# A two-layer attention, WKV and mixture-of-experts block and a diffusion block: semaphores of a stage cleared during the next stage

## The reference

```python
def first_block(x, ...):                       # 528 tokens: 16 meta tokens and x
    h = _layer_norm(concatenate([meta, x]), emb_ln_g, emb_ln_b)
    for li in range(2):
        proj = h @ w_in[li]
        c_q, c_kv, k_pe, rw = _split(proj, ...)
        y_att = _mla(c_q, c_kv, k_pe, ...)
        u = _centred_shift(rw, ...)
        y_rwkv, v_first = _rwkv_bidir(u, v_first, ...)
        mixed = concatenate([y_att, y_rwkv]) @ w_out[li]
        h = _layer_norm(DN_ALPHA * h + mixed, ...)
        ff = _hier_moe(h, ...)                 # 32 experts, two per token
        h = _layer_norm(DN_ALPHA * h + ff, ...)
    return h[:, N_META:]

def second_block(x, c, ctx, ...):
    h_lat = rms_norm(x, norm_mix) * (1 + m_lat[1]) + m_lat[0]
    ...
    ya = window_attn(...); yb = global_attn(...); yc = hgrn2_bidir(...)
    x_mix = x + m_lat[2] * merge_branches(ya, yb, yc, gates, w_branch, w_out)
    h = rms_norm(x_mix, norm_ffn) * (1 + m_lat[4]) + m_lat[3]
    return rms_norm(x_mix + m_lat[5] * conv_ffn(h, ...), norm_final)
```

## Time and profile before

| | |
|---|---|
| time, median of 3 runs | 3746.04 us (3744.92 to 3749.94) |
| the profiled execution, first to last instruction | 3735.3 us |
| PE busy | 3204.0 us, 86% |
| DVE busy | 1687.3 us, 45% |
| mean granted clock of TensorE | 0.927 of full speed |
| stages run | 20 |
| `mix_in`, layer 0 and 1 (end of second barrier to end of second barrier) | 277.5 and 282.3 us |
| `rwkv_prep` | 55.3 and 53.8 us |
| `wkv` | 302.5 and 309.1 us |
| `mix_close` | 112.4 and 111.5 us |
| `route` | 29.6 and 29.6 us |
| `experts` | 278.4 and 279.7 us |
| `combine` | 44.9 and 44.0 us |
| `scale_inputs`, `attend`, `branch_attention`, `gated_scan`, `close` | 30.9, 113.0, 301.5, 240.7, 750.9 us |

### The profile page before, as it was taken

One profiled execution on the slowest core, in us unless ns is written; L12 is line 12 of the kernel. 1 busy time (PEld: TensorE's weight loads), 2 busy tenths in 40 slices (PEclk: granted clock), 3 DMA queues, 4 the chain that ended last, 5 costly groups with the idle time before them and its releaser, 6 DMA issues. The chain is left out here.

```text
span 3735.3 us, 75687 instructions
## 1 busy us (share of the span) xinstructions
PE 3204.0 (86%) x32538; PEld 2376.1 (64%) x32538; DVE 1687.3 (45%) x3124; ACT 876.1 (23%) x1808; POOL 373.7 (10%) x530
## 2 busy tenths in 40 slices
PE   4899799986873899799986873989998899999998
PEld 0666599864442666699764442557656688878843
DVE  2344455543113344355542115445457776566611
ACT  3122322212113112323121114133353311022200
POOL 0000121001111000121001112000025400000000
PEclk7999799997996999799998996999999999999999
DMA  8210300209996110300219994110010032222221
GB/s 320 70 46 28 139 5 5 82 15 357 392 404 172 34 34 27 137 5 5 82 59 359 390 395 123 34 47 24 29 52 1 10 115 79 91 68 91 77 70 46
DMA packets 175437, 421.93 MB, mean 113 GB/s; under 512 B 25795, under 2 KB 122435, under 8 KB 146579
## 3 DMA queue, kind: packets, MB, share of 16 engines
q1 hardware_dynamic: 156147, 383.22, 27.8%
q0 software_dynamic: 8736, 17.32, 1.8%
q10 hardware_dynamic: 10240, 16.79, 1.3%
HBM read 400.55 MB, written 50.54 MB: 121 GB/s over the span
## 5 line engine op out<-in xcount | busy, mean ns | idle before, releaser
L2052 PE MATMUL ps<-e_w,e_xt 128*64 128x256 f32 x1792 | 225.7, 408 | 68.6 <-DMA e_w<-in_moe_w 67.1
L2052 PEld LDWEIGHTS ps<-e_w,e_xt 128*64 128x64 f32 x1792 | 148.8, 148 | 166.7 <-issue 78.1
L732 PE MATMUL ps<-h,win 128*128 128x264 f32 x960 | 232.8, 396 | 17.2 <-DVE pad L881 15.6
L732 PEld LDWEIGHTS ps<-h,win 128*128 128x128 f32 x960 | 180.4, 193 | 67.7 <-issue 39.1
L2159 DVE TENSOR_TENSOR e_hid<-ps,e_silu 64x256 f32<-64x256 f32 x64 | 39.4, 616 | 401.8 <-ACT e_silu L2118 401.8
L3548 PE MATMUL ps<-ff_up,wt 128*128 128x512 f32 x352 | 152.2, 592 | 0.0
L3488 PE MATMUL ps<-h_lat,wt 128*128 128x256 f32 x544 | 133.4, 388 | 15.0 <-DMA wt<-in_w_in 8.3
L1440 DVE COPY_PREDICATED inv<-level,ps 112x384 f32<-112x384 int32 x176 | 103.3, 587 | 83.2 <-PE ps L1341 74.4
L1341 PE MATMUL ps<-inv,nt 48*48 48x48 f32 x3520 | 131.4, 207 | 6.8 <-issue 5.7
L3488 PE MATMUL ps<-h_lat,w_sums 128*128 128x256 f32 x544 | 130.1, 382 | 0.0
L2071 PE MATMUL ps<-e_w,e_hid_t 128*64 128x512 f32 x448 | 110.8, 613 | 20.5 <-DMA e_w<-in_moe_w 16.9
(11 more groups left out here) (621 smaller groups left out, 6880.0 us busy)
## 6 DMA issues: line engine op xcount, KB each, us to landing
e_w<-in_moe_w SPq DMA_DIRECT2D x168, 1024.0 KB
wmod<-in_w_mod SPq DMA_DIRECT2D x24, 1024.0 KB, 14.3
early<-in_moe_w SPq DMA_DIRECT2D x24, 1024.0 KB, 13.4
wt<-in_w_up SPq DMA_DIRECT2D x22, 1024.0 KB, 5.1
y_rows<-e_y ACTq DMA_DIRECT2D x128, 128.0 KB
win<-in_w_in SPq DMA_DIRECT2D x10, 1536.0 KB, 6.6
wt<-in_w_in SPq DMA_DIRECT2D x12, 1024.0 KB, 5.1
wt<-in_w_down SPq DMA_DIRECT2D x16, 704.0 KB, 4.6
```

The costliest lines, as they stand in the source:

```text
L732: last = pe.matmul(ps[:, 7, 0:HT], lhsT=ring[(s + 1) % 2][:, i, o:o + P], rhs=k.h[:, i, h * HT:(h + 1) * HT], start=(i == 0), stop=(i == K ...
L2052: last = pe.matmul(ps[half, 2 + z, 0:EH], lhsT=xt[z][:, f, :], rhs=w[:, f, :], start=(f == 0), stop=(f == KD - 1))
```

## The change

A stage no longer has a `clear` block of its own, unless it must. Its semaphores are kept in `k.spent` until the next stage ends. That stage adds, behind SP's own code, a second stretch for SP that clears them one by one, and then closes its block with the one barrier. The next stage's semaphores have other numbers, because the old ones are given back only then. Stages that keep the old form (one barrier, the clears dealt out, a second barrier) are those that use the fixed set or semaphores that outlive them (`experts`, `combine`, `attend`, `gated_scan`) and those marked `settle=True` (`prelude`, ahead of the loop, and `close`, the last). The seven others are `mix_in`, `rwkv_prep`, `wkv`, `mix_close` and `route`, run twice, and `scale_inputs` and `branch_attention`, run once.

```diff
@@ class Stage @@
     def __exit__(self, *exc):
+        k = self.k
+        pool = [s for n, s in zip(self.names, self.sems) if n in k.pool_sems]
+        sems = [s for n, s in zip(self.names, self.sems) if n not in k.pool_sems] + self.also
+        spent, k.spent = k.spent, None
+        if exc[0] is None and spent is not None:
+            @self.b.sync
+            def _(sp):
+                for s in spent[0]:
+                    sp.sem_clear(s)
         self.block.__exit__(*exc)
+        if spent is not None:
+            spent[1].__exit__(None, None, None)
+        if exc[0] is None and not (pool or self.also or self.settle):
+            k.spent = (sems, self.stack)
+            return
         if exc[0] is None:
-            with self.k.nc.Block() as clear:
-                pool = [s for n, s in zip(self.names, self.sems) if n in self.k.pool_sems]
-                sems = [s for n, s in zip(self.names, self.sems) if n not in self.k.pool_sems] + self.also
+            with k.nc.Block() as clear:
```

More of the change, by code:

```diff
@@ L117, in __init__, with stage @@
         self.pool_sems = {}
+        self.spent = None
     def sb(self, name, shape, dt=F32, stack=None, side="left"):
         return (stack or self.top).enter_context(self.nc.sbuf_tensor(name, shape, dt, side=side))
-    def stage(self, *names, also=()):
-        return Stage(self, names, also)
+    def stage(self, *names, also=(), settle=False):
+        return Stage(self, names, also, settle)
     def pool_dma_sems(self, *names):
@@ L131, with __init__ @@
 class Stage:
-    def __init__(self, k, names, also=()):
-        self.k, self.names, self.also = k, names, list(also)
+    def __init__(self, k, names, also=(), settle=False):
+        self.k, self.names, self.also, self.settle = k, names, list(also), settle
     def __enter__(self):
@@ L353, in prelude @@
                      "strip_turned", "modded", "gained", "pre_chain", *[f"x_in{j}_" for j in range(NC1)],
-                     *[f"wmod_in{i}" for i in range(RING)]) as (
+                     *[f"wmod_in{i}" for i in range(RING)], settle=True) as (
                 block, blanked, consts_in, par_in, pos_in, pos_set, grid_in, c_done, ps_clear, centred, emb_squared, emb_root,
@@ L3435, in close @@
                  "x_scaled", "hl_made", "side_made", "silu_done", "gated", "f_squared", "f_summed", "f_root",
-                 "f_scaled", "o_turned", "o_kept", "o_stored", "dve_chain", *[f"w_in{z}" for z in range(RING)]) as (
+                 "f_scaled", "o_turned", "o_kept", "o_stored", "dve_chain", *[f"w_in{z}" for z in range(RING)],
+                 settle=True) as (
             block, p6_made, p7_made, p3_made, made, p1_kept, split, t_made, u2_made, u34_made, assembled, posted,
```

## The result

The changed kernel takes 3727.35 us (median of 4 runs, 3721.26 to 3729.23) against 3745.48 for the kernel before in the same comparison (4 runs, 3741.45 to 3749.94). The ratio is 0.995, with a 95% interval of 0.9938 to 0.9963.

A forecast was written before the change was run, and what follows sets the result against it. It took the seams between stages, where all five engines stand still, as on the path whichever engine bounds a stage. Seams 11.9 less `route` 0.6 gave 11.3 us off 3746.0: 3734.7 us, range 3729.5 to 3740.0.

The forecast's parts named there:

- The seams' sum: At twelve of 20 stage ends, the stretch from first to second barrier release on PE goes: 11.9 us saved.
- The cost in `route`: SP's 21 added clears stand behind its wait for stores, making SP last at the barrier in layer 0: 0.6 us.
- The lower bound: In `route`, added cost 0 if the stores land some 1.2 us ahead of DVE in both layers.
- The covers: In the stages other than `route`, SP reaches the barrier early, so its added clears cost nothing.
- The first rival: Behind `wkv`, shorter PE idle time keeps the clock up in `mix_close`: 4.2 us more saved, 3730.5 us; chance 0.13.
- The second rival: In `wkv`, clock drops shift both layers into the worse pattern: 6.6 us lost, 3741.3 us; chance 0.14.
- The third rival: At the twelve seams, the pause had covered code fetch: 1.2 us each, 14.4 us cost, 3749.1 us; chance 0.03.
- From span to median: For the whole run, the median of runs was taken as 10.7 us above the profiled execution, 3735.3 us.
- What it named as its own test: Over all stages, the prediction is wrong if the sum of lengths falls by under 7.5 us or over 16.

The follow-up runs named there:

- Experiment 2: Kernel before with every seam's clears done twice: 3759.09 us, ratio 1.0034; changed kernel with an empty second barrier kept at twelve seams: 3736.31 us, 0.998; repeated 3740.13, 0.9981.

## Why the prediction was right or wrong, point by point

**The seams' sum, 11.9 us: right.** It measured 12.2, and the 0.3 between is rounding. Experiment 2 shows that such a microsecond counts as one.

**The cost in `route`, 0.6 us: it measured nothing.** SP, with its 21 clears, was at the barrier 0.7 and 1.2 us ahead of DVE in the first trace of the changed kernel and 0.4 to 1.4 us ahead of the release in all eight `route` ends of four traces. The clears did cost SP 1.2 us, as reckoned; but the stores that it waits for landed earlier against DVE than in the two places of the earlier trace rows. Why they did was not tried. The lower bound, 0, was the right end.

**The covers: right.** SP's clears vanish in `rwkv_prep`, `wkv`, `mix_close`, `attend`, `gated_scan` and `experts`: in the first trace of the changed kernel SP is at these barriers 16 us or more ahead of the release. `experts` moved by 0.6 us.

**The first rival, the clock gives more back: right in kind, and the step that failed.** It was priced at 4.2 us in one stage, given a chance of 0.13 and kept out of the forecast. `mix_close` gave back 3.0 of these 4.2. What was missing is the second place: the earlier trace rows looked at the short stretch behind one seam, and I had not looked behind the others. The 2.7 us of `rwkv_prep` had a sign in the kernel before, in whose trace its two runs start at 0.54 and 0.66 with 54.4 and 52.7 us. The argument used against it, that the last matmuls of `wkv` are thin anyway, is no reason: they were as thin after. The mis-sized term is thus the clock's share, taken as 0 in the forecast, where 7.6 ± 1.1 us were measured by the means and 6.5 ± 1.3 by the ratios. Some 0.6 of it is the shorter time outside the span, and 5.7 are found in the two stages; the rest has not been traced.

**The second rival, the clock takes some: refuted for the median.** `wkv` stayed at 300.7 to 302.3 us in layer 0 of all four traces of the changed kernel and took 301.0 to 309.5 in layer 1, so both layers at 309 never came; it is scatter, as the prediction itself argued against it.

**The third rival, code fetch: refuted.** At each of the twelve seams of the changed kernel, in all four traces, some engine is at work within 0.1 us of the release. PE is at eight of them; at the end of `mix_in` it starts after 0.7 us and at that of `route` after some 11, both as in the kernel before.

**From span to median: a step that was wrong and hid itself.** The forecast took the profiled execution's distance from the median, 10.7 us, as a constant. That execution took some 3738 us with the time outside its span, 10 below the mean of 3747.6; the changed kernel's profiled execution is 3721.26 against a mean of 3727.6. Both lie at the low end of the scatter. Since only the difference of 11.3 was laid on the median, the error did no harm here; but stretches read from such a trace are those of a short execution, perhaps with fewer starts at the lower clock than the mean has.

**What it named as its own test**, a sum of the stages' lengths that falls by over 16 us, was just not met by the profiled pair (15.9), and was met by the mean spans of all executions (19.4).

## What to carry to other kernels

A pause in which all engines stand still costs its whole length, which is read from release to release, and it can cost again, by the clock that PE has behind it: look at the granted clock and the length of the first 10 to 15 us behind every such pause, in all instances of the stage, and where the same stage starts at different clocks, price each seam with that difference before giving it a small chance. Clear semaphores with one instruction over a range of numbers, or where the engine has time; dealing single clears over engines is bound by PE at 0.12 us each. And take a forecast's base from means over executions, since a single trace may lie at either end of the scatter.

## What the runs showed of the hardware that was not expected

- One range clear on SP takes 90 ns for 39 semaphores, and a whole second barrier is 0.33 us.
- PE's clock answers to a microsecond more or less of pause, where PE is idle for 1.5 to 3 us in all: seams of 1.15 and 0.33 us ahead of `rwkv_prep` and none at all give means of 54.0, 53.7 and 52.6 us for the same 160 matmuls, in two, two and four traces.
- A float32 matmul of 128x512 has two rows in the trace, up to 1.19 us each in a seam; two such matmuls took 3.75 us where the granted clock was 0.50 and 1.95 us where it was 1.00.
- More work in a kernel shortened the rest of it: matmuls that nobody reads, at 20 seams, made the stages 11 us faster, at a price of 35 us for themselves.
